# A two-layer diffusion trunk step: the opening reordered, transposes of the identity in TensorE's queue, and two of three weight products in one matmul

## The reference

```python
for l in range(DEPTH):                       # 2
    hc = modulate(xc, norm_mix[l], mc[0], mc[1])     # rmsnorm(x) * (1 + scale) + shift
    # layer 0: retention (4 heads, both directions); layer 1: windowed attention with a sink
    xc = xc + mc[2] * yc                             # gate
    hc = modulate(xc, norm_ffn[l], mc[3], mc[4])
    xc = xc + mc[5] * conv_ffn(hc, ffn_w_in[l], ffn_conv_w[l], ffn_conv_b[l], ffn_w_out[l])
```

## Time and profile before

| what | value |
|---|---|
| times of three runs | 2034.37, 2031.87, 2025.85 us (median 2031.87) |
| the profiled execution | 2033.87 us, its span 2032.1 us |
| TensorE busy | 1980.2 us of 11280 matmuls |
| DVE, ACT, POOL busy | 996.7, 662.3, 780.4 us |
| the chain that ended last | TensorE 89%, DVE 3%, ACT 2%, POOL 2% |
| granted TensorE clock, mean | 0.993 |

### The profile page before, as it was taken

How to read it: one execution, slowest core, us unless ns; L and a number is a source line. 1 busy time by engine, 2 the same in 40 slices (tenths; PEclk the granted TensorE clock), 3 DMA queues, 4 the chain that set the end, 5 groups by cost and what they waited for, 6 DMA issues and landing times.

```text
span 2032.1 us, 29546 instructions
## 1 busy us (share of the span) xinstructions
PE 1980.2 (97%) x11280; PEld 1695.2 (83%) x11280; DVE 996.7 (49%) x1333; ACT 662.3 (33%) x1321; POOL 780.4 (38%) x535
## 2 busy tenths in 40 slices
PE   6999999999999999999999999998999999999998
PEld 3787988788788878998998998894568998998996
DVE  2422530442253157662564475665634772674475
ACT  5432223213222225331232234335535332232232
POOL 3333333234323425333223334436854433333332
PEclk9999999999999999999999999998999999999999
DMA  8421332322233213432432221510013322222221
GB/s 334 166 73 63 125 114 73 121 95 86 73 120 113 75 36 125 156 110 77 152 120 100 73 83 62 184 63 6 1 53 125 115 73 83 73 72 83 73 73 52
DMA packets 53558, 195.75 MB, mean 96 GB/s; under 512 B 5968, under 2 KB 7376, under 8 KB 52432
## 3 DMA queue, kind: packets, MB, share of 16 engines
q1 hardware_dynamic: 48096, 174.68, 24.4%
q10 hardware_dynamic: 5360, 19.65, 2.6%
HBM read 187.23 MB, written 7.08 MB: 96 GB/s over the span
## 4 chain that ended last, share of the span: by engine, by line
PE 89%; DVE 3%; ACT 2%; POOL 2%; issue 2%; DVEq 1%; DMA 0%; POOLq 0%; ACTq 0%
PE ps L463 36%; PE ps L508 20%; PE ps L478 16%; PE ps L695 4%; PE ps L724 3%; PE ps L540 2%; DVE front L1514 1%; PE ps L414 1%; ACT pr L1303 1%; POOL pr L1487 1%; POOL h_l L1411 1%; PE ps L418 1%; PE ps L561 1%; PE ps L529 1%; PE ps L902 1%
## 5 line engine op out<-in xcount | busy, mean ns | idle before, releaser
L1368 POOL TENSOR_TENSOR w_l<-raw,w_h 128x1024 fp32r<-128x1024 f32 x232 | 568.6, 2454 | 1029.4 <-ACT w_h L1004 1029.4
L463 PE MATMUL ps<-h_h,w_h 128*128 128x384 f32 (+1 forms) x1696 | 530.1, 313 | 0.0
L463 PE MATMUL ps<-h_h,w_l 128*128 128x384 f32 (+1 forms) x1696 | 523.9, 309 | 0.0
L463 PE MATMUL ps<-h_l,w_h 128*128 128x384 f32 (+1 forms) x1696 | 523.8, 309 | 0.0
L1004 ACT CAST w_h<-raw 128x1024 fp32r<-128x1024 f32 x232 | 245.5, 1060 | 528.6 <-PE ps L508 274.5
L463 PEld LDWEIGHTS ps<-h_h,w_h 128*128 128x128 f32 x1696 | 321.5, 190 | 12.6 <-issue 10.8
L463 PEld LDWEIGHTS ps<-h_l,w_h 128*128 128x128 f32 x1696 | 321.6, 190 | 2.5 <-issue 2.4
L463 PEld LDWEIGHTS ps<-h_h,w_l 128*128 128x128 f32 x1696 | 321.4, 189 | 0.0
L1774 DVE SCALAR_TENSOR_TENSOR cc<-ca,vec,cc 128x641 f32<-128x641 f32 x88 | 219.5, 2494 | 14.3 <-issue 13.1
L478 PE MATMUL ps<-w_h,h_h 128*128 128x512 f32 x480 | 188.7, 393 | 1.0 <-issue 1.0
L478 PE MATMUL ps<-w_l,h_h 128*128 128x512 f32 x480 | 187.2, 390 | 0.0
(11 more groups left out here) (220 smaller groups left out, 2866.6 us busy)
## 6 DMA issues: line engine op xcount, KB each, us to landing
raw<-stream_dram SPq DMA_DIRECT2D x312, 512.0 KB, 3.3
first_w<-first_dram SPq DMA_DIRECT2D x16, 512.0 KB, 15.3
gate<-gate_b_dram ACTq DMA_DIRECT2D x4, 1024.0 KB, 4.8
S<-state_dram ACTq DMA_DIRECT2D x4, 1024.0 KB, 7.5
new_state_dram<-st_out ACTq DMA_DIRECT2D x8, 512.0 KB, 5.1
xt<-x_dram ACTq DMA_DIRECT2D x5, 512.0 KB, 9.7
y_dram<-front SPq DMA_DIRECT2D x5, 512.0 KB, 2.6
rope_t<-rope_t_dram ACTq DMA_DIRECT2D x4, 512.0 KB, 3.5
```

What stands on the lines that cost most here:

```text
L463: mm = nc.tensor.matmul(ps[:, banks + half, 0:width(half)], w, x[:, k, lo_hi(half)], start=(k == 0 and n == 0), stop=(k == KT - 1 and n == 2))
L1368: nc.gpsimd.tensor_tensor(w_l[:, r, :], raw[:, s, :], w_h[:, r, :].bitcast(F32), ALU.subtract).then_inc(raw_used[s], 1)
```

## The change

**One matmul for two products.** `h_h` and `h_l` become halves of one tensor `hx`. A new function `sum_tile` takes the place of `feature_tile` in both FFNs and in attention (92 tiles; retention's 14 stay). In the first bank it multiplies `w_h` by 256 columns of `h_h` and 256 of `h_l` at once (512 columns, a moving operand in two pieces that fill the bank's two halves), and `w_l` by the 256 columns of `h_h` into the first half. The sum of the halves is then made outside: ACT copies the second half, DVE adds the first half to it. The second bank is as before. The first bank is now free when DVE has added (`a_sum`, `aq_sum`), the second when ACT has copied (`a_evac`, `aqk_evac`).

```diff
+            def sum_tile(b, j, i, banks, free):
+                s = weights(b, j, i)
+                free(0)
+                both = ps[:, banks, :].rearrange("p (a t) -> p a t", a=2)
+                for k in range(KT):
+                    wh, wl = (w[:, s, k * P:(k + 1) * P] for w in (w_h, w_l))
+                    if k < KT - 1:
+                        nc.tensor.matmul(both, wh, hx[:, :, k, 0:HALF], start=(k == 0), stop=False)
+                    nc.tensor.matmul(both[:, 0], wl, h_h[:, k, 0:HALF], start=False, stop=False)
+                nc.tensor.matmul(both, wh, hx[:, :, KT - 1, 0:HALF], start=False, stop=True)
+                free(1)
...
                                     def free(half, w=w, n=n):
                                         if half == 0:
+                                            if n == 1:
+                                                pe.wait_ge(a_low[l], w + 1)
+                                            else:
+                                                pe.wait_ge(a_sum[l], 2 * n + w - 3 + 4 * i)
+                                        else:
                                             pe.wait_ge(a_evac[l], 2 * n + w + 1 + 4 * i)
...
-                                    nc.scalar.copy(a[:, 1:1 + NCTX], ps[:, 2 * w, 0:NCTX])
-                                    nc.scalar.copy(a[:, NCTX + 2:NCTX + 2 + CUT], ps[:, 2 * w, NCTX:HALF])
+                                    half = slice(0, HALF) if n == 0 else slice(HALF, 2 * HALF)
+                                    nc.scalar.copy(a[:, 1:3 + HALF].rearrange("p (c t) -> p c t", c=2)[:, :, 0:P],
+                                                   ps[:, 2 * w, half].rearrange("p (c t) -> p c t", c=2)
+                                                   ).then_inc(a_low[l], 1)
...
+                                    if n > 0:
+                                        dve.wait_ge(a_low[l], 2 * n + w + 1 + 4 * i)
+                                        begin = a[:, 1:3 + HALF].rearrange("p (c t) -> p c t", c=2)[:, :, 0:P]
+                                        V.tensor_tensor(begin, ps[:, 2 * w, 0:HALF].rearrange("p (c t) -> p c t", c=2),
+                                                        begin, ALU.add).then_inc(a_sum[l], 1)
+                                        dve.drain()
...
+                if j >= 2:
+                    dve.wait_ge(aq_low, j + 1)
+                    ctx_to = aq[:, j, 0:NCTX] if j < 8 else ak[:, j - 8, 0:NCTX]
+                    V.tensor_tensor(ctx_to, ps[:, 2 * (j % 2), 0:NCTX], ctx_to, ALU.add)
+                    V.tensor_tensor(lat[:, 0:CUT], ps[:, 2 * (j % 2), NCTX:HALF], lat[:, 0:CUT],
+                                    ALU.add).then_inc(aq_sum, 1)
```

```diff
-            for t in range(2):
-                norm_turn(0, t, (0,))
+            warm(12)
             ada_first(0)
+            warm(6)
+            norm_turn(0, 0, (0,))
             ada_turn(0, 1)
+            warm(6)
+            norm_turn(0, 1, (0,))
+            warm(6)
+            ada_first(1, range(0, 4))
+            warm(8)
             norm_turn(0, 2, (0,))
-            ada_first(1)
+            warm(6)
+            ada_first(1, range(4, KT))
+            warm(6)
             ada_turn(0, 2)
-            ada_first(2, range(0, 4))
+            warm(20)
             for t in range(3, TT):
                 norm_turn(0, t, (0,))
+            warm(8)
...
-                first_pair(b, 0, 0, range(0, 2))
-                ada_first(2, range(4, KT))
-                first_pair(b, 0, 0, range(2, 4))
+                first_pair(b, 0, 0, range(0, 4))
+                ada_first(2)
+                first_pair(b, 0, 1, range(0, 2))
                 ada_turn(0, 3)
-                first_pair(b, 0, 1, range(0, 1))
+                first_pair(b, 0, 1, range(2, 4))
                 ada_first(3)
-                first_pair(b, 0, 1, range(1, 3))
+                warm(6, 7)
                 ada_turn(0, 4)
-                first_pair(b, 0, 1, range(3, 4))
...
             for t in range(TT):
                 norm_f(0, t, 0)
-                if t == 2:
-                    ada_copy(None, 2, 0, 0)
+                if t == 0:
+                    slot, ready = SEG["ret0"].split(1, 0)
+                    dve.wait_ge(hi_ready[slot], ready)
+                    V.tensor_tensor(w_l[:, slot, :], raw[:, slot, :], w_h[:, slot, :].bitcast(F32),
+                                    ALU.subtract).then_inc(raw_used[slot], 1)
             norm_lo(0, 2, 0)
+            ada_copy(None, 2, 0, 0)
```

```diff
+                if u == UNITS - 1:
+                    pe.wait_ge(aolo_done, EARLY_PAIRS)
+                    for half in range(2):
+                        pe.wait_ge(ae_done, 2 * UNITS - 1 + half)
+                        out_early(SEG["att_o"], 0, range(2 * half, 2 * half + 2))
                 if u == UNITS:
-                    pe.wait_ge(ae_done, 2 * UNITS)
-                    pe.wait_ge(aolo_done, EARLY_PAIRS)
-                    out_early(SEG["att_o"], 0)
                     out_early(SEG["att_o"], 1, range(0, 2))
```

## The result

The changed kernel takes **2018.73 us** (median of five executions, 2016.55 to 2019.81) against 2028.21 for the kernel before in the same session: a ratio of 0.9941, 95% interval 0.9928 to 0.9955. The forecast was 2012.4, with 2005 to 2019 as its own range and 2024 as the end with rival B. So the sign held and the time lies inside the range, and the forecast's gain of 19.5 us was about twice the 9.5 measured here. In three later sessions the kernel before lay between 2024.4 and 2035.2 (63 executions, median 2029.6). The changed kernel, here and once more later, lay between 2016.2 and 2022.6 (11 executions, median 2018.31, mean 2018.4).

The account below looks back on a forecast made before the run. TensorE, busy 1980.2 of 2032.1 us, was taken to bound the kernel. Terms -8.5 + 0.4 - 6.0 - 4.9 - 0.5 = -19.5 us gave 2012.4 against the median of 2031.9; range 2005 to 2019, with B to 2024.

Parts of the forecast that it names:

- rival B: Merged matmul's two pieces pay separately, merge gives nothing: 2020.9 us, chance 0.15; with the skill's 2.5 ns surcharge 2019.1.
- Merge, -8.5: First bank of 92 tiles: eight merged 512-column matmuls make the half 2.77 us, 0.093 less, saving 8.5 us.
- DVE's sum, +0.4: DVE's new sum costs nothing in the FFN; attention's q and k sums, partly overlapping, add 0.4 us.
- I cost it at nothing in the FFN: FFN: DVE's sum with drain, put at 0.5 us, hides in waits, with 3.8 us to spare before the bank is needed.
- rival C: DVE becomes the FFN's bound and TensorE waits at tile starts: +5.9 us, 2037.8, chance 0.08.
- Opening, -6.0: Opening with new order and filler transposes ends at 56.5 instead of 62.51 us; ends of the gain 9.6 and 0.
- What they buy is the clock: Opening: filler transposes lie on the path but bring 2.4 GHz instead of 1.2, assumed to rise at 21 us.
- Attention's end, -4.9: 24 early projection matmuls fill pauses of 2.17 and 0.93 us and avoid a 2.2 us slow stretch, less 0.4 waiting.
- the lower bound of 2.7: Attention's end: the gain left, 2.7 us, if the slow stretch comes anyway.
- After retention, -0.5: First transposes move ahead by one token tile but wait 1.5 us for scaled `x`: gain 0.5 us, ends -1.5 and +2.3.
- rival A: Opening: the clock does not rise before block 1 ends; opening gains 1.6 us, in all -15.1: 2016.8, chance 0.15.
- the prediction's last sign: Whole kernel: a gain below 10 us or above 27 would mean a term is wrong, not only its size.

Follow-up runs that it names:

- no_fill: Changed kernel with all 84 transposes of the identity left out of the opening, its new order kept: 2018.11 us.
- lean_fill: Changed kernel without the 26 transposes of the identity between the first turn and block 1's end, block 1 multiplied in one piece: 2018.34 us.
- old_order: Changed kernel with the whole opening of the kernel before, no transposes of the identity: 2019.86 us, from 2016.60 to 2026.36.
- old_order_fill: Changed kernel with the opening of the kernel before plus 30, 8 and 6 transposes of the identity: 2019.80 us, from 2018.68 to 2021.77.

## Why the forecast was right in sign and twice too large

- **Merge, -8.5.** Mis-sized. The step "the half takes 2.77 us, 0.093 less" held (2.78). The step left unsaid, that the rest of the tile stays as it was, did not: 0.02 us came back in the second half, so a tile gave 0.064 and not 0.093. 92 tiles give 5.9 by the traces; undoing six of eight merges, which brought a tile back to 7.03, cost 5.1 in the medians. Rival B is refuted. So are the 1.8 us that the surcharge of the Trainium skill ("TensorE: Matmul & The Clock Gate", "Wait — 56ns, not 53.3ns?") would have given.
- **DVE's sum, +0.4.** This step failed. "I cost it at nothing in the FFN" looked only at TensorE's waits for DVE, where it was right (rival C did not come; the sum took 0.42 us, but 0.82 with its drain and not 0.5). The price went by another road: DVE's shifted step, POOL's longer subtraction, a raw chunk, a modulation block. Removing the sum gave 2.4 us. The Trainium skill ("SBUF — State Buffer", "Who interferes with whom") says that DVE, in its two-port modes, and GpSimd hold a shared pair of ports as a lock, and whoever starts first has it for the whole instruction. The trace agrees in direction: L1846 began 0.12 us ahead of POOL and ran 0.49 us into its subtraction, which took 0.34 longer. I had used such collisions as a cover for DVE and not asked what they do to POOL.
- **Opening, -6.0.** Between the two profiled executions it was right in size (-6.65), by errors that cancelled: block 0 1.5 us late, the clock 3 us early. But the sum stood against one execution, 2033.87, and a median of three, while executions of the kernel before reach from 2024.4 to 2035.2. It was one whose clock came late. By the medians the new opening is worth 1.6 us, by the means 2.2, and in the best executions nothing; with eight executions of the old order, spread over 10 us, neither figure is firm. "What they buy is the clock" is not borne out: all 84 transposes can go at no cost that can be measured. That the order keeps a late clock cheap is the reading that fits these runs; it was not shown by itself. That the best executions with the old order had an early clock is inferred from their times (2016.6 to 2018.4); none of them was traced. Of a late clock itself the Trainium skill ("TensorE: Matmul & The Clock Gate", "What's actually happening") says that the moment of the rise varies from run to run, there by 0.5 us either way. These traces show it, and by more: with the same instructions the fast level was there at 18 us in one and at 11.6, and again at 23.7, in another.
- **Attention's end, -4.9.** The pauses were right, and so was the lower bound of 2.7: measured 2.8. The 2.2 us for the slow stretch were charged as certain, from one execution; in the trace without the early projection it did not come.
- **After retention, -0.5.** No experiment; the traces agree (47.62 us from retention's last projection to the first FFN tile before, 47.1 after).

The sum by what was measured: merge -5.9, its sum +2.4, opening -1.6, attention -2.8, retention -0.5, in all -8.4. The medians differ by 11.3, or by 9.5 in the first session. The remaining 3 us are not assigned. The changed kernel's two sessions have medians 1.0 us apart and the kernel before's four sessions up to 1.6, so that such differences can add up to it. The traces say where it may lie. From the first feature tile to the end of the span it is 1964.8 us before (2032.1 - 67.26) and 1955.6 to 1957.6 in six traces that have the change behind the opening (the changed kernel twice, no_fill, lean_fill, old_order, old_order_fill). That is 7.2 to 9.2 us, so that 2.1 to 4.1 of the 11.3 are left for the opening. The part before rests on one trace.

The nearest time to the result was the 2019.1 of rival B in the form with a surcharge of 2.5 ns, then rival A's 2016.8. Neither mechanism was there: the merge gave 5.9 and not 1.8 us, and the clock did rise before block 1's end. The forecast's time was 6.3 us off and its gain 8 to 10, all its larger errors going the same way. The difference is luck: the median of three from which it starts, 2031.9, lies 2.3 us above that of the 63 later executions. That the result falls 0.3 us inside the forecast's own upper end is luck too. By the prediction's last sign, a gain below 10 us, a term had to be wrong and not only its size. The 9.5 of the first session meets that, the 11.3 of all sessions does not; the term that was wrong in kind is DVE's sum in the FFN.

Two sums of the prediction do not come out of its own terms. With the opening and attention at their ends the range is 2008.8 to 2020.6 and not 2005 to 2019. And rival C counts 44 pairs where 42 have the new sum, which gives 2035.6 and not 2037.8.

## What to carry to other kernels

Before a stall of the opening is priced, ask how many executions have it: the spread of the times shown (8 us against a gain of 19) was the sign that the profiled one need not be the usual one. When work is added to an engine beside the critical path, follow it past the engine's own slack to whoever it collides with, and to the transfers that this neighbour releases. And when a tile is added to a kernel, put it last, or compare a row of untouched matmuls first: here eight bytes a partition cost as much as all edits had gained.

## What was not expected of the hardware

- Matmuls of 512 columns take 0.2333 us instead of 0.2268 from start to start when the SBUF tile from which TensorE loads its 128x128 operand starts 8 bytes later (56.00 against 54.44 us for 240). Which alignment is enough was not tried. Feature tiles, whose two operands both lie ahead of the shift, stayed at 83.63 us for twelve.
- A matmul whose moving operand has two pieces of 256 columns takes 0.230 us, 0.003 more than a contiguous one of 512.
- Nine traced executions with the same instructions in the opening differ by 4.7 us in when its first feature tile comes (58.5 to 63.2 us); two of one kernel differ by 2.6.
